# Softmax attention in units of four heads: score maxima scaled bank by bank, and the values' products ordered by key tile

## The reference

```python
s = einsum('qe,ke->qk', q, k) * scale + mask
m = max(s, axis=-1)                    # with the sink's logit among them, where there is one
p = exp(s - m); den = sum(p)
o = einsum('qk,ke->qe', p / den, v)
```

## Time and profile before

| what | value |
|---|---|
| median of 3 runs | 1165.59 us (1165.52 to 1165.68) |
| profiled execution, span | 1167.2 us |
| mean granted TensorE clock | 0.993 of full |
| busy: PE / PEld / DVE / ACT | 1117.7 / 914.2 / 895.2 / 741.7 us |
| instructions: PE / DVE / ACT | 5515 / 1462 / 1313 |
| read from HBM | 219.13 MB, 189 GB/s over the span |

### The profile page before, as it was taken

One profiled execution on the slowest core, in us unless ns is written; L12 is line 12 of the kernel. 1 busy time (PEld: TensorE's weight loads), 2 busy tenths in 40 slices (PEclk: granted clock), 3 DMA queues, 4 the chain that ended last, 5 costly groups with the idle time before them and its releaser, 6 DMA issues.

```text
span 1167.2 us, 14667 instructions
## 1 busy us (share of the span) xinstructions
PE 1117.7 (96%) x5515; PEld 914.2 (78%) x5515; DVE 895.2 (77%) x1462; ACT 741.7 (64%) x1313; POOL 0.2 (0%) x4
## 2 busy tenths in 40 slices
PE   7999999999999999998999999999989999999996
PEld 5788787888787788887877787877778778787774
DVE  4756857777768867766668868999977886899996
ACT  5746565655656665556355556888845655688883
POOL 0000000000000000000000000000000000000000
PEclk9999999999999999999999998999999999999998
DMA  8654454453443455633542416999926322499991
GB/s 288 239 181 144 145 177 137 157 179 109 145 140 114 164 197 172 201 108 106 184 145 108 145 38 190 348 360 359 360 91 214 130 99 87 157 357 357 364 349 39
DMA packets 131841, 221.25 MB, mean 190 GB/s; under 512 B 6144, under 2 KB 77360, under 8 KB 131760
## 3 DMA queue, kind: packets, MB, share of 16 engines
q1 hardware_dynamic: 127920, 213.21, 53.2%
q10 hardware_dynamic: 3840, 6.98, 1.8%
HBM read 219.13 MB, written 1.05 MB: 189 GB/s over the span
## 4 chain that ended last, share of the span: by engine, by line
PE 74%; DVE 14%; ACT 7%; issue 3%; DMA 2%; ACTq 0%; DVEq 0%
PE bank L487 20%; PE bank L489 20%; PE bank L488 20%; PE bank L786 3%; PE bank L851 3%; DVE wL L440 2%; ACT wH L432 2%; ACT S L806 2%; DMA ring<-in_w_mem_kv 1%; PE bank L636 1%; PE bank L2277 1%; PE bank L832 1%; DVE mx L795 1%; PE bank L2326 1%; PE bank L1738 1%
## 5 line engine op out<-in xcount | busy, mean ns | idle before, releaser
L440 DVE TENSOR_TENSOR wL<-ring,wH 128x1024 fp32r<-128x1024 f32 (+1 forms) x316 | 375.9, 1213 | 138.5 <-ACT wH L432 137.3
L432 ACT ACTIVATE wH<-ring 128x1024 fp32r<-128x1024 f32 (+1 forms) x316 | 320.5, 1047 | 32.3 <-PE bank L489 19.8
L487 PE MATMUL bank<-wH,hTH 128*128 128x512 f32 (+2 forms) x592 | 237.9, 402 | 3.0 <-DVE wL L440 2.1
L488 PE MATMUL bank<-wL,hTH 128*128 128x512 f32 (+2 forms) x592 | 232.1, 392 | 0.0
L489 PE MATMUL bank<-wH,hTL 128*128 128x512 f32 (+2 forms) x592 | 231.9, 392 | 0.0
L487 PEld LDWEIGHTS bank<-wH,hTH 128*128 128x128 f32 x592 | 111.5, 188 | 27.9 <-DVE wL L440 3.5
L489 PEld LDWEIGHTS bank<-wH,hTL 128*128 128x128 f32 x592 | 111.5, 188 | 24.8
L488 PEld LDWEIGHTS bank<-wL,hTH 128*128 128x128 f32 x592 | 111.6, 189 | 23.1 <-issue 0.5
L487 PE MATMUL bank<-wH,xgH 128*128 128x512 f32 x256 | 105.2, 411 | 0.0
L488 PE MATMUL bank<-wL,xgH 128*128 128x512 f32 x256 | 101.9, 398 | 0.0
L489 PE MATMUL bank<-wH,xgL 128*128 128x512 f32 x256 | 101.9, 398 | 0.0
(11 more groups left out here) (297 smaller groups left out, 1863.0 us busy)
## 6 DMA issues: line engine op xcount, KB each, us to landing
ring<-in_w_in_a SPq DMA_DIRECT2D x44, 1024.0 KB, 4.9
ring<-in_w_out SPq DMA_DIRECT2D x20, 1024.0 KB, 4.8
ring<-in_w_down SPq DMA_DIRECT2D x20, 1024.0 KB, 6.3
ring<-in_w_gate SPq DMA_DIRECT2D x36, 512.0 KB, 5.1
ring<-in_w_up SPq DMA_DIRECT2D x36, 512.0 KB, 6.5
ring<-in_w_in_b SPq DMA_DIRECT2D x14, 1024.0 KB, 5.0
ring<-in_w_mem_kv SPq DMA_DIRECT2D x8, 1024.0 KB, 7.1
ring<-in_w_in SPq DMA_DIRECT2D x8, 1024.0 KB, 5.4
```

The source lines that it names most:

```text
L432: act.e.activation(quarter_parts(q)[0], quarter_in_ring(q), COPY).then_inc(w_high, 1)
L440: dve.e.tensor_tensor(lo, quarter_in_ring(q), hi.bitcast(F32), SUB).then_inc(w_low, 1)
L487: pe.e.matmul(o, a[0], b[0], start=first, stop=False)
L488: pe.e.matmul(o, a[0], b[1], start=False, stop=False)
```

## The change

In `dve_max`, the step for the sink and the scaling move into the loop over the banks, each on its bank's slice of the four heads, and each scaling signals `max` with its bank's number. `act_exp` waits for `max` of the bank that the head is in. In `pe_turn` the transposes of heads 0 and 1 wait for `exp` 0 and those of heads 2 and 3 for `exp` 1. In `pe_values` the loops change places: key tile 0 of all four heads is multiplied behind the first copy, and key tile 1 behind the second. The values are waited for first. Since four accumulations are now open in one bank, only the very first matmul has the start flag, which clears the whole bank's state.

```diff
         def dve_max(u):
+
             nb, each = small(4, "nb", u.name), 4 // u.n_banks
             for x in range(u.n_banks):
+                h = slice(each * x, each * x + each)
                 dve.wait_ge(at("scores", u.name, x))
-                dve.follow().tensor_reduce(u.mx[:, each * x:each * x + each], score_bank(u, x), AX, MAX).then_inc(*dve.did())
-            if u.sink is not None:
-                dve.wait_ge((d_rows, 160))
-                dve.follow().scalar_tensor_tensor(u.mx, u.mx, u.scale, u.sink, MUL, MAX).then_inc(*dve.did())
-            dve.follow().tensor_scalar(nb, u.mx, -1.0 if u.sink is not None else -u.scale, None, MUL).then_inc(*dve.did("max", u.name))
+                dve.follow().tensor_reduce(u.mx[:, h], score_bank(u, x), AX, MAX).then_inc(*dve.did())
+                if u.sink is not None:
+                    dve.wait_ge((d_rows, 160))
+                    dve.follow().scalar_tensor_tensor(u.mx[:, h], u.mx[:, h], u.scale, u.sink[:, h], MUL, MAX).then_inc(*dve.did())
+                dve.follow().tensor_scalar(nb[:, h], u.mx[:, h], -1.0 if u.sink is not None else -u.scale, None, MUL).then_inc(
+                    *dve.did("max", u.name, x))
 
         def act_exp(u):
             n, nb = u.nk * P, small(4, "nb", u.name)
-            act.wait_ge(at("max", u.name))
+            each = 4 // u.n_banks
             for s in range(4):
-                each = 4 // u.n_banks
+                act.wait_ge(at("max", u.name, s // each))
                 act.e.activation(u.S[:, s, 0:n], score_bank(u, s // each)[:, s % each, :], EXP, bias=nb[:, s:s + 1], scale=u.scale,
                                  accum_out=u.den[:, s:s + 1]).then_inc(*act.did("exp", u.name, s // 2))
...
         def pe_turn(u):
             for kt in range(u.nk):
                 b = att_bank(("turn", u.name, kt), at("emit", u.name) if kt == 0 else at("PT", u.name, 1))
-                pe.wait_ge(at("exp", u.name, 1))
                 for s in range(4):
+                    pe.wait_ge(at("exp", u.name, s // 2))
                     tr = pe.e.transpose(b.t[:, s * P:(s + 1) * P], u.S[:, s, kt * P:(kt + 1) * P], ident)
                 tr.then_inc(*pe.did("turn", u.name, kt))
...
         def pe_values(u):
             b = bank_of["turn", u.name, 0]
-            pe.wait_ge(*[at("PT", u.name, kt) for kt in range(u.nk)], *u.v_ready)
-            for s in range(4):
-                for kt in range(u.nk):
-                    mm = pe.e.matmul(b.t[:, s * u.dv:(s + 1) * u.dv], u.PT[:, kt, s, :], u.vh(s, kt), start=kt == 0, stop=kt == u.nk - 1)
+            pe.wait_ge(*u.v_ready)
+            for kt in range(u.nk):
+                pe.wait_ge(at("PT", u.name, kt))
+                for s in range(4):
+                    mm = pe.e.matmul(b.t[:, s * u.dv:(s + 1) * u.dv], u.PT[:, kt, s, :], u.vh(s, kt), start=kt + s == 0, stop=kt == u.nk - 1, skip_group_check=True)
             mm.then_inc(*pe.did("values", u.name))
```

## The result

The changed kernel takes 1164.55 us at the median (1159.94 to 1172.1), the kernel before, run beside it, 1166.34 us (1164.99 to 1177.02). The two medians lie 1.8 us apart. The ratio, close to that of the two means (1164.54 to 1168.58), is 0.9966, with a 95% interval of 0.9951 to 0.9981: 4.0 us faster, between 2.2 and 5.7. Forecast were 5.8 us and 1159.8 us. The direction is right, the stops went where I said, and some of the gain was lost again to a lower TensorE clock. The profiled execution of the changed kernel has a span of 1164.7 us at a mean clock of 0.987; that of the kernel before had 1167.2 us at 0.993.

What follows compares the result with a forecast made beforehand. TensorE was taken to bound the kernel, except where layer B's chain alternates between VectorE and ScalarE. Savings of 1.6 + 0.5 + 3.5 + 0.2 = 5.8 us from 1165.6 gave 1159.8 us, range 1156.3 to 1164.8.

Steps and rivals of the forecast that it cites:

- the bound of 1163.3: Whole kernel: times from 1163.3 to 1167.9 us count as the same, some 0.2% (2.3 us); same had chance 0.13.
- Layer A, 1.6 and 0.5: Layer A's first and fourth attention: TensorE's stops at 121.36 and 268.65 go, saving 1.6 and 0.5 us.
- Layer B, 3.5: Layer B's attention: four units gain 0.70 each (2.8), the last unit's products start 0.66 earlier; 3.5 us together.
- Rival 1: Layer B's VectorE-ScalarE loop does not move; only the products' order gains, 2.6 us in all: 1163.0 us; chance 0.16.
- rival 2: Whole kernel: nothing arrives, local gains fall into waits behind them: 1165.6 us; chance 0.09.
- Mixing layers, 0.1 each: Both mixing layers: products starting on the first copy give 0.5, VectorE's extra work costs 0.4; net 0.1 us each.
- New waits at nothing: TensorE's transposes and products: at most 56 new waits, nearly all already met, taken as 0; ceiling 3.9 us.
- rival 3: Low parts behind the maxima: VectorE becomes the bound, extra instructions cost up to 4.9 us: 1170.5 us; chance 0.06.
- rival 4: TensorE's clock: one half-speed fall more or fewer, 1.7 us each: 1161.5 or 1158.1 us; chance 0.09.
- my signs of being wrong: Low parts' idle vanishes in attention, third exponential waits, 657.16 comes over 0.5 us later relative to 549.2, or new half-speed stretch.

Runs made afterwards that it cites:

- the loop part alone: Kernel before with only the scaling by bank and the exponentials' wait by bank, sink units included; transposes and products as before: 1171.47 us, ratio 1.0029.
- the loop part without the sink units: Kernel before with scaling and exponentials by bank only in units without a sink; transposes and products as before: 1166.43 us, ratio 0.9979.

## Why the prediction was right, and where it was not

**The number.** The measured median, 1164.55 us, lies inside the stated range by 0.25 us and outside the forecast's own range of 1157.5 to 1162; by the bound of 1163.3 it would even count as the same. The local sum was right and the total came out higher by a cost that the sum had at nothing, the clock. That the range still held it is partly luck.

**Layer A, 1.6 and 0.5.** Right. Unheld, TensorE was to start the first products at 119.75; this execution began its attention 0.68 us earlier (102.04 against 102.72 for the first mask, which the change has no part in: the repeated profile has 102.57), so 119.07 was due, and 118.98 is measured. The stop of 268.65 is gone too: the fourth attention's transposes stand at 265.79 with no idle time before them.

**Layer B, 3.5.** Right in kind and a little low. A and B together were to give 5.6 and gave 6.37. Of the 0.8 more, 0.36 is a stop that I had not looked at: the latent transposes waited 0.53 us before and wait 0.17 now, on TensorE's timeline of the two kernels:

```profile
595.05 0.87 PE L1727 MATMUL bank<-const,arena 128*128 128x128 f32 x6 [0.53 <-DVE arena L1925]
```

```profile
588.00 0.87 PE L1731 MATMUL bank<-const,arena 128*128 128x128 f32 x6 [0.17 <-DVE arena L1929]
```

Rival 1 (the loop does not move) is out: the loop part alone gave 3.35 us in its profile, 4.1 with the fall at 378 us allowed for. So is rival 2 (nothing arrives), since the latent transposes come 7.05 us earlier, 6.37 of it counted from the first mask.

**Mixing layers, 0.1 each.** The sum was right (0.16), its terms partly. The extra 0.4 of VectorE was exact, 0.40 in the loop part alone and 0.39 by leaving it out. The products' order was to give 0.5. Alone it gave 0.17, and the loop part without the sink units gave 0.01; all parts together, with the sink units as before, give 0.55 (95.32 against 95.87). So the parts need each other there: 0.55 less 0.39 is the 0.16. That the terms cancelled to the right sum is luck in part, as the 0.5 was put down to the products' order alone.

**New waits at nothing.** Right: the two transposes' waits alone left both mixing layers within 0.01 us.

**VectorE as the bound (rival 3).** Out for the change: idle before the low parts fell only from 139.8 to 134.1 us. Doubling the scalings cost what later exponentials cost, about half of what a VectorE at its limit would have.

**The step that failed is rival 4**, by its weight and its size. I wrote that the trace showed stops of 1.6 us in attention with no fall at all, and gave the clock little. That was one execution. Over many, falls come in some and not in others, at the same places. Among the experts one is worth 1.5 us, near my 1.7, but it is 0.8 at 378 us, 3.2 at 929 us and 5.1 in the kernel before with idle matmuls; and the runs of the changed kernel have a median clock lower by 0.003 than the kernel before's. The local sum came out at 6 to 7 us at an equal clock; 4.0 arrived by the ratio, 3.2 by the medians of all runs. Of my signs of being wrong, this one appeared: a new half-speed stretch of the clock. The Trainium skill ("Perfetto Trace Analysis", Matmul Optimizations) says that the matmul engine scales its power by utilization and wants matmuls back to back; the rows agree in part. The falls at 378 and 929 us begin right after a stop of TensorE, and the stretches behind the routers lost theirs when their stops were filled. But the changed kernel's fall at 1010.8 us has no idle time before it, only a run of products of 4 columns, on TensorE's timeline:

```profile
1008.80 1.95 PE L2288 MATMUL bank<-SG,OH 128*128 128x4 f32 x16
1010.60 0.61 PE L487 MATMUL bank<-wH,xgH 128*128 128x512 f32 x1
```

**What of the clock is shown, and what not.** Shown side by side with the whole change (1164.3 to 1160.8 us), and less surely with the loop part alone (1171.5 to 1166.4): scaling the sink units by bank costs 3.5 to 5 us of whole time, while its own work costs 0.8 us, and the rest goes with a mean clock 0.003 to 0.006 lower. Open: by what path those instructions lower the clock. The obvious link, the longer stop before the output flips, was shortened by only 0.11 us when the clock came back, and in the profiles part of the loss stands behind the second router, whose own work is the same in all versions. Nor is the long fall of the changed kernel's profile behind them: it begins at 928.9 us, and the first sink unit with two banks of that layer comes to VectorE only later:

```profile
936.35 0.69 DVE L797 TENSOR_REDUCE mx<-bank 128x2 f32<-128x512 f32 x1
937.07 0.16 DVE L800 SCALAR_TENSOR_TENSOR mx<-mx,rows 128x2 f32<-128x2 f32 x1
```

A mixing layer has a long fall in three of the five profiles whose sink units scale by bank, and in one of the eight others, which is too few to settle it. No run here separates the place of a stop from its length.

## What to carry to other kernels

Split a small step by bank where its consumer stands on the path, and only there: in units without a sink, one more instruction of 0.17 us freed ScalarE 0.7 us earlier; in units with a sink, where VectorE was itself the chain, the same split cost 0.39 us in each mixing layer and went with a lower clock besides. When an experiment's windows and its time disagree, read the granted clock of every run before doubting the theory, and compare runs at an equal clock, by all their runs and not by a few. A part of a change can look slower alone (1.0029) and still be worth about half of the gain.

## What the runs showed of the hardware

- With one core at work and the same program, runs spread by 12 us (1159.94 to 1172.1) and their times follow the mean granted clock: 0.993 gave about 1161 us, 0.990 gave 1164.5, 0.981 gave 1172.1, in the changed kernel.
- The clock falls to its 1.2 GHz level for some 3 to 14 us in stretches where TensorE is otherwise busy, behind stops as short as the 0.30 us at 928.58, or with no idle time before it (1010.8). The changed kernel's first profile has the fall at 929 us and its second has none in that layer (98.91 and 95.78 us).
- A fall of 3.4 us costs 1.5 us among the experts (188.95, 187.50 and 186.02 us with three, two and one) and 0.8 us at 378 us.
- Filling stops with idle matmuls spared the falls behind the routers (none in three profiles, against nine of ten) and only one of three at the second layer's entry. In the kernel before the time as a whole did not change (0.9984, 0.9960 to 1.0009), and in its profile a long fall came elsewhere.
